# Attention outputs made as features: values, scores and transposes of three pairs in one stop of TensorE

## The chip, the cores and the metric

One NeuronCore of a Trainium2 chip runs the whole program in one launch. The metric is the device time in microseconds. The kernel before takes 2653.07 us (median of 3 runs, 2652.22 to 2653.91). TensorE is called PE here, VectorE DVE, ScalarE ACT, GpSimd POOL and the engine that issues the DMAs SP.

## The reference

Two transformer blocks run one after the other on 256 tokens with 2048 features. The first is a gated recurrence with convolutions and an MLP; the second, which most of the change touches, is

```
h = rms_norm(x, norm1_g)
aq, ak, av, bu, bg, cq, ck, cv = split(h @ w_in)            # 512 x5, 1024, 128, 128 columns
out_a = dilated_mixture(rms(aq), rms(ak), av)               # 8 heads of 64, each with its own keys and values
out_b = silu(layer_norm(causal_conv31(bu * sigmoid(bg))))   # 512 channels, 31 taps
out_c = band_attention(rms(cq), rms(ck), cv, sinks)         # 16 query heads, 2 key/value heads of 64
x = x + concat(out_a, out_b, out_c) @ w_out
x = x + (silu(rms_norm(x) @ w_gate) * (rms_norm(x) @ w_up)) @ w_down
```

An attention output is softmax(q k^T + mask) v for each head: o = P v / rowsum(P), where P is the exponential of the scores less their row maximum. The two LayerNorms of the first block are x -> (x - mean) * rstd * g + b over the 2048 features.

## The kernel before

Weights stream from HBM in pieces of 128 x 1024 numbers through a ring of four slots. Each float32 weight piece is split in two parts for the fast matmul: ACT writes the rounded upper part w_hi (L894, `split`), DVE the rest w_lo (L1365, `lo`), and PE multiplies both. A piece frees its slot when PE is done with it, and PE, ACT and DVE each have their order written out by hand, with semaphores between them.

The second block's attention runs beside the projections of `w_in` and `w_out`. Pieces of this part are numbered m = 0 to 59. For m = 0 to 43 a piece is 12 matmuls of 512 columns (L498 to L500); for m = 44 to 59 it is a `narrow_piece` of `w_out` (L831, L835), which reads the attention outputs. Before piece m each engine calls its own `beside(m)`, which holds the small work that has come due. The names to know are:

- `PAIRS`: 12 pairs of heads, eight of kind C (with sinks) and then four of kind A. Pair n is started at piece 16 + 3n (`PAIRS_AT`, `EVERY`), and `pair_at(m, late)` says which pair is due `late` pieces after its start.
- For a pair: `scores` on PE (late 0), `prepare` on DVE (late 0; adds the mask, takes the row maximum), `exps` on ACT (late 1), `transposes` on PE (late 3) and `turned_probs` on ACT (late 3), `values` on PE and `scale_out` on DVE (late 5), `turn_out` on PE and its split in mix_hi and mix_lo by ACT and DVE (late 7).
- `taps` on DVE: the 124 steps of the 31-tap convolution (31 for each of four tiles), spread over pieces 3 to 43 by `taps_by(m)`. At m = 44 DVE adds up the result (`part_of`, L1934, L1936), and PE sums it over the channels at m = 45 (`column_sum`, L618).
- `head_variance` and `norm_heads` on DVE at m and m + 1 for m in `HEADS_END` = 4, 12, 20, 28, 36; PE turns the normalised heads at m + 3 (L709) and has to wait for `norm_heads`.
- In the loop over m DVE does `scale_out`, then `lo` of piece m + 3, then `beside(m)`: first mix_lo, then `prepare`, the heads and the taps. Its queue is in order, so each of these stands behind the others.

The LayerNorms of the first block end on a chain PE (turns the normalised tiles, L600), DVE and ACT (gain and shift, `features` and `scaled`), ACT (`high`), DVE (`low`), PE (next matmul). While the chain runs PE does matmuls with zeros (`keep_busy`, L529).

## Time and profile before

| | |
|---|---|
| runs, median | 2653.07 us (2652.22 to 2653.91) |
| the profiled execution's own time | 2652.17 us |
| its span | 2650.4 us |
| granted TensorE clock | 0.999 |
| PE busy | 2640.4 us, 100% of the span |
| DVE busy | 1750.5 us, 66% |
| ACT busy | 1347.2 us, 51% |
| DMA | 494 MB, mean 186 GB/s |

The time of the profiled execution is 1.8 us above its span: what lies around it. Busy times are over the whole span; the stretches matter here, since the change touches some 200 us. In rows of a timeline the first number is a start in us from the span's beginning, the second how long the merged instructions took; a float32 matmul leaves two records, so six matmuls stand as x12 or as several rows of x2. Matmuls overlap, so the distance between two starts tells what one costs.

### The profile page before, as it was taken

What the parts mean: (1) busy time and instruction counts of PE and PEld (TensorE: products, weight loads), DVE (VectorE), ACT (ScalarE), POOL (GpSimd) and SP (SyncE); (2) the same over time, 40 slices, a digit from 0 to 9 for tenths busy, and PEclk for the clock granted to TensorE, in tenths of its full rate; (3) what the DMA queues carried; (4) which work ended last, traced back from release to release, by engine and by line L of the source; (5) the groups of instructions that cost most, each with busy time, mean ns of one, the idle gap of its engine ahead of it and who ended that gap; (6) DMA issues with size and microseconds to landing.
All of it is one profiled execution on the core that took longest, in us unless ns stands there. A gap on an engine that the chain in (4) does not pass through costs nothing.

```text
span 2650.4 us, 40578 instructions
## 1 busy us (share of the span) xinstructions
PE 2640.4 (100%) x14407; PEld 2291.4 (86%) x14407; DVE 1750.5 (66%) x1875; ACT 1347.2 (51%) x1540; POOL 36.6 (1%) x30
## 2 busy tenths in 40 slices
PE   9999999999999999999999999999999999999999
PEld 8888888888888888888888888889888888888888
DVE  7788877544454655555555568997666666666667
ACT  5767765444444544444444445566554444444444
POOL 0000000000000100000000001000100000000000
PEclk9999999999999999999999999999999999999999
DMA  7555555555555455555555554433555555555554
GB/s 266 182 186 188 187 189 192 200 181 190 202 195 199 165 183 195 178 191 200 194 178 193 199 191 157 168 136 136 175 191 187 188 189 189 190 190 190 190 190 167
DMA packets 133881, 494.01 MB, mean 186 GB/s; under 512 B 14864, under 2 KB 15376, under 8 KB 133776
## 3 DMA queue, kind: packets, MB, share of 16 engines
q1 hardware_dynamic: 133776, 492.62, 54.5%
q8 instruction: 65, 1.06, 0.2%
q14 instruction: 40, 0.33, 0.0%
HBM read 490.46 MB, written 2.10 MB: 186 GB/s over the span
## 4 chain that ended last, share of the span: by engine, by line
PE 95%; DVE 3%; issue 1%; ACT 1%; DMA 0%; DVEq 0%; SPq 0%; ACTq 0%
PE ps_b L389 18%; PE ps_a L389 18%; PE ps_b L400 10%; PE ps_a L400 10%; PE ps_b L498 6%; PE ps_b L500 6%; PE ps_b L499 6%; PE ps_a L498 5%; PE ps_a L499 5%; PE ps_a L500 5%; PE ps_b L831 1%; DVE w_lo L1365 1%; PE ps_b L835 1%; DVE bconv L1866 1%; DVE gates L1511 1%
## 5 line engine op out<-in xcount | busy, mean ns | idle before, releaser
L1365 DVE TENSOR_TENSOR w_lo<-w_raw,w_hi 128x1024 fp32r<-128x1024 f32 (+1 forms) x908 | 1120.6, 1251 | 731.7 <-ACT w_hi L894 722.1
L894 ACT ACTIVATE w_hi<-w_raw 128x1024 fp32r<-128x1024 f32 (+1 forms) x908 | 967.7, 1076 | 1130.1 <-PE ps_b L500 242.4
L389 PE MATMUL ps_b<-xx,w_hi 128*128 128x512 f32 x1184 | 288.6, 393 | 3.4 <-DVE xx L1682 1.8
L389 PE MATMUL ps_a<-xx,w_hi 128*128 128x512 f32 x1120 | 269.1, 391 | 0.0
L389 PEld LDWEIGHTS ps_b<-xx,w_hi 128*128 128x128 f32 x1184 | 217.6, 189 | 46.9 <-ACT w_hi L894 3.4
L389 PEld LDWEIGHTS ps_a<-xx,w_hi 128*128 128x128 f32 x1120 | 205.8, 188 | 39.9
L389 PE MATMUL ps_a<-x,w_hi 128*128 128x512 f32 x704 | 165.9, 390 | 0.0
L389 PE MATMUL ps_b<-x,w_hi 128*128 128x512 f32 x704 | 165.5, 390 | 0.0
L400 PEld LDWEIGHTS ps_b<-xx,w_lo 128*128 128x128 f32 x1184 | 152.8, 192 | 5.8
L400 PE MATMUL ps_b<-xx,w_lo 128*128 128x256 f32 x1184 | 155.5, 283 | 0.0
L389 PEld LDWEIGHTS ps_b<-x,w_hi 128*128 128x128 f32 x704 | 130.8, 188 | 26.2
L389 PEld LDWEIGHTS ps_a<-x,w_hi 128*128 128x128 f32 x704 | 130.6, 188 | 26.1
L400 PEld LDWEIGHTS ps_a<-xx,w_lo 128*128 128x128 f32 x1120 | 142.3, 191 | 4.8 <-DVE w_lo L1365 0.4
L400 PE MATMUL ps_a<-xx,w_lo 128*128 128x256 f32 x1120 | 144.7, 283 | 0.0
L498 PE MATMUL ps_b<-w_hi,xx 128*128 128x512 f32 (+1 forms) x320 | 124.0, 388 | 0.0
L500 PE MATMUL ps_b<-w_hi,xx 128*128 128x512 f32 (+1 forms) x320 | 121.5, 380 | 0.0
L499 PE MATMUL ps_b<-w_lo,xx 128*128 128x512 f32 (+1 forms) x320 | 121.4, 379 | 0.0
L498 PE MATMUL ps_b<-w_hi,ff 128*128 128x512 f32 x256 | 99.9, 390 | 0.0
L500 PE MATMUL ps_b<-w_hi,ff 128*128 128x512 f32 x256 | 99.6, 389 | 0.0
L499 PE MATMUL ps_b<-w_lo,ff 128*128 128x512 f32 x256 | 99.6, 389 | 0.0
L498 PE MATMUL ps_a<-w_hi,ff 128*128 128x512 f32 x256 | 99.6, 389 | 0.0
L499 PE MATMUL ps_a<-w_lo,ff 128*128 128x512 f32 x256 | 99.6, 389 | 0.0
(311 smaller groups left out, 3960.7 us busy)
## 6 DMA issues: line engine op xcount, KB each, us to landing
w_raw<-w_dram SPq DMA_DIRECT2D x836, 512.0 KB, 3.3
w_raw<-w_dram SPq DMA_DIRECT2D x72, 640.0 KB, 4.0
zz<-x_dram SPq DMA_DIRECT2D x8, 256.0 KB, 4.7
x_res<-x_dram SPq DMA_DIRECT2D x4, 512.0 KB, 4.6
out_dram<-res SPq DMA_DIRECT2D x3, 512.0 KB, 2.8
out_dram<-res SPq DMA_DIRECT2D x4, 128.0 KB, 2.1
const<-const_dram SPq DMA_DIRECT2D x1, 449.0 KB, 5.8
prm<-prm_dram SPq DMA_DIRECT2D x1, 308.0 KB, 5.4
```

What stands on the lines that cost most here:

```text
L389: last = nc.tensor.matmul(group[:, j, :], w_hi[:, r, o * P:o * P + P], moving(src, at + k), start=begins and k == 0, stop=not begins and k ...
L400: last = nc.tensor.matmul(group[:, j, 0:S], w_lo[:, r, o * P:o * P + P], moving(src, at + k)[:, 0:S], start=begins and k == 0, stop=not be ...
L498: nc.tensor.matmul(dst, x_hi, hi, start=k == 0 and not begun, stop=False)
L499: nc.tensor.matmul(dst, x_hi, lo, start=False, stop=False)
L500: last = nc.tensor.matmul(dst, x_lo, hi, start=False, stop=k == kt - 1)
L831: nc.tensor.matmul(banks[:, j // 2, (j % 2) * S:(j % 2) * S + S], w_hi[:, r, cols], mix_tile(k)[:, half_at:half_at + S], start=False, stop ...
L835: last = nc.tensor.matmul(banks[:, j // 2, (j % 2) * S:(j % 2) * S + S], w_lo[:, r, cols], mix_tile(k)[:, 0:S], start=False, stop=k == 3 a ...
L894: act.activation(w_hi[:, r, 0:width], w_raw[:, r, 0:width], ACT.Copy).then_inc(hi_done, 1)
L1365: dve.tensor_tensor(w_lo[:, r, 0:width], w_raw[:, r, 0:width], w_hi[:, r, 0:width].bitcast(F32), ALU.subtract).then_inc(lo_even if r % 2 = ...
L1511: own.done(dve.tensor_tensor_scan(gates[:, hd, way, 0, order], aa[:, way, hd, order], tt[:, way, hd, order], 0.0, ALU.mult, ALU.add))
L1866: ins = dve.scalar_tensor_tensor(y, x, column("cv_w", n), y, ALU.mult, ALU.add)
```

## The change

The attention outputs are made with features in the partitions, so they need no transpose after them. For that the probabilities are divided by their sum before they are turned (`scale_probs` on DVE replaces `scale_out`), and `values` takes the values as the stationary operand (128 keys x 64 features) and the turned probabilities as the moving one (128 columns). The two heads of a pair write partitions 0 to 63 and 64 to 127 of the last quarters of the banks GA 2 and GA 3; `turn_out`, the tile `on` and two semaphores go. On PE the values of pair n - 3, the scores of pair n and the transposes of pair n - 2 stand together, in one stop in three pieces (two later at the end: `values_at`). DVE does `scale_probs` and `prepare` before its `lo`. The taps are spread anew: none at pieces 12 to 14, 88 from piece 15 on, where there were 72 from piece 16 on. In the LayerNorms the transposes go in the order 0, 2, 1, 3 with a semaphore after tile 2 of the first block, ACT does its first `high` before its first `scaled`, and 4 of the 26 `keep_busy` matmuls that ran there go.

```diff
             turn_normed(0, 1)
-            keep_busy(4, GB[:, 0, :])
+            keep_busy(2, GB[:, 0, :])
...
-                    for j in range(SN):
+                    for j in (0, 2, 1, 3):
                         last = nc.tensor.transpose(normed_tile(b, j)[:, t * P:t * P + P], zt[:, t, b, j * P:j * P + P], ident)
+                        if (b, t, j) == (0, 1, 2):
+                            last.then_inc(first_turned, 1)
...
             turn_normed(1, 1)
-            keep_busy(5, GB[:, 0, :])
+            keep_busy(3, GB[:, 0, :])
...
+        def values_at(m):
+
+            n, last = pair_at(m, 9), pair_at(m, 8)
+            return last if last is not None and last >= 9 else n if n is not None and n < 9 else None
...
             def transposes(n):
-                pe.wait_ge(exp_done, n + 1)
+                pe.wait_ge(p_scaled, n + 1)
...
             def values(n):
-                for hd in range(2):
-                    part = slice(64 * hd, 64 * hd + 64)
-                    p_t = probs_t[:, n % 2, hd, :]
-                    nc.tensor.matmul(GA[:, 0, 64 * hd:64 * hd + 64], p_t[:, 0:P], vt[:, 0, v, part], start=True, stop=True)
...
+                for keys, block in ((0, 0), (0, 1), (1, 1)):
+                    at = (keys + block) * P
+                    for hd in range(2):
+                        part = slice(64 * hd, 64 * hd + 64)
+                        last = nc.tensor.matmul(GA[part, 2 + block, 3 * P:4 * P], vt[:, keys, v, part],
+                                                probs_t[:, n % 2, hd, at:at + P], start=keys == 0, stop=keys == block)
                 last.then_inc(o_psum, 1)
...
-                n = pair_at(m, 3)
-                if n is not None:
-                    transposes(n)
-                n = pair_at(m, 5)
+                n = values_at(m)
                 if n is not None:
                     values(n)
-                n = pair_at(m, 7)
-                if n is not None:
-                    turn_out(n)
                 n = pair_at(m, 0)
                 if n is not None:
                     scores(n)
+                n = pair_at(m, 6)
+                if n is not None:
+                    transposes(n)
...
             def first_blocks(n, q):
+                act.wait_ge(first_kept, n + 1)
+                high(n, 0, 1).then_inc(first_hi, 1)
                 act.wait_ge(norm_turned[n], 1)
                 scaled(n, 0, 1).then_inc(first_kept1, 1)
-                act.wait_ge(first_kept, n + 1)
                 act.wait_ge(first_kept1, n + 1)
-                high(n, 0, 1).then_inc(first_hi, 1)
...
-                return max(0, min(4 * TAPS2, 4 * (m - 2) if m < 16 else 52 + (72 * (m - 15) + 27) // 28))
+                return max(0, min(4 * TAPS2, 4 * (m - 2) if m < 12 else 36 if m < 15 else 36 + (88 * (m - 14) + 28) // 29))
...
-            def scale_out(n):
+            def scale_probs(n):
...
+                for blk, cols in ((0, slice(0, P)), (1, slice(P, 3 * P))):
+                    part = probs[:, b, :, cols]
+                    last = dve.tensor_tensor(part, part, rsum[:, b, blk, :].unsqueeze(2).to_broadcast(
+                        [P, 2, cols.stop - cols.start]), ALU.mult)
+                last.then_inc(p_scaled, 1)
...
             for m in range(MIX_END):
-                n = pair_at(m, 5)
+                n = pair_at(m, 2)
                 if n is not None:
-                    scale_out(n)
+                    scale_probs(n)
+                n = pair_at(m, 0)
+                if n is not None:
+                    prepare(n)
```

On PE, before, the work of pairs 2, 3 and 4 stands at three pieces in turn (values of 2 at piece 27, transposes of 3 and scores of 4 at 28, the turn of output 2 at 29), each between ordinary matmuls:

```order
L759 MATMUL ps_a<-vt,probs_t 128x64
L498 MATMUL ps_b<-w_hi,xx 128x512
...
L742 MATMUL ps_a<-const,probs 128x128 x6
L729 MATMUL ps_a<-ckt,cqt 128x128
L730 MATMUL ps_a<-ckt,cqt 128x256
L729 MATMUL ps_a<-ckt,cqt 128x128
L730 MATMUL ps_a<-ckt,cqt 128x256
L498 MATMUL ps_b<-w_hi,xx 128x512
...
L766 MATMUL ps_a<-const,on 128x128 x2
```

Of the change, the stop of PE at piece 28 (values of pair 1, scores of 4, transposes of 2) is

```order
L504 MATMUL ps_b<-w_hi,xx 128x512
L761 MATMUL ps_a<-probs_t,vt 64x128 x6
L733 MATMUL ps_a<-ckt,cqt 128x128
L734 MATMUL ps_a<-ckt,cqt 128x256
L733 MATMUL ps_a<-ckt,cqt 128x128
L734 MATMUL ps_a<-ckt,cqt 128x256
L746 MATMUL ps_a<-const,probs 128x128 x6
L502 MATMUL ps_b<-w_hi,xx 128x512
```

The three visits became one; the six value matmuls write 64 partitions and 128 columns where they wrote 128 and 64, and the two output transposes are gone.

DVE before, pieces 22 to 24 (w_lo is `lo`, probs<-ps_a and peak are `prepare`, bconv the taps, mixc the lower part of an output, rsum and on are `scale_out`):

```order
L1882 TENSOR_TENSOR probs<-ps_a,const 128x768
L1885 TENSOR_REDUCE peak<-probs 128x2
L1886 TENSOR_REDUCE peak<-probs 128x2
L1892 TENSOR_SCALAR negm<-peak,prm 128x2 x2
L1866 SCALAR_TENSOR_TENSOR bconv<-bpad,prm,bconv 128x256 x2
L1365 TENSOR_TENSOR w_lo<-w_raw,w_hi 128x1024
L1389 TENSOR_TENSOR mixc<-ps_a,mixc 128x256
L1866 SCALAR_TENSOR_TENSOR bconv<-bpad,prm,bconv 128x256 x3
L1900 TENSOR_TENSOR rsum<-rsum,sink 128x4
L1902 RECIPROCAL rsum<-rsum 128x4
L1907 TENSOR_TENSOR on<-ps_a,rsum 128x256
L1365 TENSOR_TENSOR w_lo<-w_raw,w_hi 128x1024
```

DVE of the change, from the end of piece 23 into piece 25:

```order
L1859 SCALAR_TENSOR_TENSOR bconv<-bpad,prm,bconv 128x256 x3
L1894 TENSOR_TENSOR rsum<-rsum,sink 128x4
L1896 RECIPROCAL rsum<-rsum 128x4
L1900 TENSOR_TENSOR probs<-probs,rsum 128x2x128
L1900 TENSOR_TENSOR probs<-probs,rsum 128x2x256
L1358 TENSOR_TENSOR w_lo<-w_raw,w_hi 128x1024
L1859 SCALAR_TENSOR_TENSOR bconv<-bpad,prm,bconv 128x256 x3
L1875 TENSOR_TENSOR probs<-ps_a,const 128x768
L1878 TENSOR_REDUCE peak<-probs 128x2
L1879 TENSOR_REDUCE peak<-probs 128x2
L1885 TENSOR_SCALAR negm<-peak,prm 128x2 x2
L1358 TENSOR_TENSOR w_lo<-w_raw,w_hi 128x1024
```

The division of 256 numbers in each partition became one of 768 in two instructions, `prepare` stands ahead of `lo`, and three taps stand in each piece where there were two or three.

## Rows read from the trace of the kernel before

**Rows 1.** The page: busy us (share of the span) and instructions
```profile
PE 2640.4 (100%) x14407; PEld 2291.4 (86%) x14407; DVE 1750.5 (66%) x1875; ACT 1347.2 (51%) x1540; POOL 36.6 (1%) x30
```
**Rows 2.** Windows, pieces 16 to 43 and 44 to 59: stretch, length, busy by engine, clock, DMA
```profile
1700.27:1808.90 108.63, 108.63 (x606) 88.65 (x605) 101.09 (x195) 71.40 (x148) 0.00 (x0) 1.00 0.41 144
1808.90:1867.33 58.43, 58.43 (x486) 57.05 (x485) 36.88 (x53) 34.27 (x58) 0.00 (x0) 1.00 0.40 139
```
**Rows 3.** Timeline of PE: the values of one pair (piece 21)
```profile
1716.40 0.39 PE L500 MATMUL ps_b<-w_hi,xx 128*128 128x512 f32 x1
1716.63 0.33 PE L756 MATMUL ps_a<-vt,probs_t 128*128 128x64 f32 x2
...
1718.20 0.39 PE L499 MATMUL ps_b<-w_lo,xx 128*128 128x512 f32 x1
```
**Rows 4.** Timeline of PE: transposes and scores (piece 22)
```profile
1720.74 0.82 PE L742 MATMUL ps_a<-const,probs 128*128 128x128 f32 x6
1721.48 0.50 PE L729 MATMUL ps_a<-ckt,cqt 64*128 64x128 f32 x4
1721.81 0.61 PE L730 MATMUL ps_a<-ckt,cqt 64*128 64x256 f32 x4
...
1722.69 0.40 PE L499 MATMUL ps_b<-w_lo,xx 128*128 128x512 f32 x1
```
**Rows 5.** Timeline of PE: the turn of an output (piece 26)
```profile
1737.69 0.38 PE L766 MATMUL ps_a<-const,on 128*128 128x128 f32 x2
...
1738.14 0.40 PE L499 MATMUL ps_b<-w_lo,xx 128*128 128x512 f32 x1
```
**Rows 6.** Timeline of DVE, pieces 22 to 24
```profile
1725.75 0.95 DVE L1882 TENSOR_TENSOR probs<-ps_a,const 128x768 f32<-128x768 f32 x1
...
1728.05 0.87 DVE L1866 SCALAR_TENSOR_TENSOR bconv<-bpad,prm,bconv 128x256 f32<-128x256 f32 x2
1728.84 1.22 DVE L1365 TENSOR_TENSOR w_lo<-w_raw,w_hi 128x1024 fp32r<-128x1024 f32 x1
...
1730.31 1.27 DVE L1866 SCALAR_TENSOR_TENSOR bconv<-bpad,prm,bconv 128x256 f32<-128x256 f32 x3
1731.50 0.15 DVE L1900 TENSOR_TENSOR rsum<-rsum,sink 128x4 f32<-128x4 f32 x1
...
1732.37 1.23 DVE L1365 TENSOR_TENSOR w_lo<-w_raw,w_hi 128x1024 fp32r<-128x1024 f32 x1
```
**Rows 7.** Timeline of DVE at pieces 12 and 13
```profile
1689.72 1.23 DVE L1365 TENSOR_TENSOR w_lo<-w_raw,w_hi 128x1024 fp32r<-128x1024 f32 x1
1690.85 1.22 DVE L1915 TENSOR_REDUCE hsum<-hsq 128x16 f32<-128x1024 f32 x1
...
1692.20 1.67 DVE L1866 SCALAR_TENSOR_TENSOR bconv<-bpad,prm,bconv 128x256 f32<-128x256 f32 x4
...
1694.92 0.25 DVE L1924 RECIPROCAL hrn<-hsd 128x16 f32<-128x16 f32 x1
...
1696.34 1.66 DVE L1866 SCALAR_TENSOR_TENSOR bconv<-bpad,prm,bconv 128x256 f32<-128x256 f32 x4
```
**Rows 8.** Timeline of PE: turn of the heads at piece 15, with its idle time
```profile
1696.48 1.09 PE L709 MATMUL ps_b<-const,hnb 128*128 128x128 f32 x8 [0.88 <-DVE hnb L1928]
```
**Rows 9.** Timeline of DVE at piece 44
```profile
1810.25 1.23 DVE L1365 TENSOR_TENSOR w_lo<-w_raw,w_hi 128x1024 fp32r<-128x1024 f32 x1 [0.38 <-ACT w_hi L894]
```
**Rows 10.** Timeline of PE: the column sum at piece 45
```profile
1813.71 0.65 PE L618 MATMUL ps_a<-bpart,ones 128*128 128x256 f32 x2
```
**Rows 11.** Timeline of ACT: its first gain and shift in the second LayerNorm
```profile
1600.88 0.56 ACT L1071 ACTIVATE res<-ps_a,prm 128x256 f32<-128x256 f32 x1 [0.58 <-PE ps_a L600]
```
**Rows 12.** Timeline of PE in the second LayerNorm: zero matmuls, and a wait behind them
```profile
1601.47 1.34 PE L529 MATMUL ps_b<-zero 128*128 128x512 f32 x5
1602.71 0.70 PE L389 MATMUL ps_b<-xx,w_hi 128*128 128x512 f32 x2
...
1611.23 0.47 PE L389 MATMUL ps_b<-xx,w_hi 128*128 128x512 f32 x1 [1.81 <-DVE xx L1682]
```

More of the change, by code:

```diff
@@ L225, in build @@
             sem(n) for n in ("score_psum", "score_out", "peak_ready", "exp_done"))
-        pt_psum, pt_out, o_psum, o_scaled, o_turned = (
-            sem(n) for n in ("pt_psum", "pt_out", "o_psum", "o_scaled", "o_turned"))
+        p_scaled, pt_psum, pt_out, o_psum = (sem(n) for n in ("p_scaled", "pt_psum", "pt_out", "o_psum"))
         mix_hi, mix_lo = sem("mix_hi"), sem("mix_lo")
@@ L737, in transposes @@
                 if n >= 2:
-                    pe.wait_ge(mix_lo, n - 1)
+                    pe.wait_ge(mix_lo, n - 1 if n < 10 else n)
                 for hd in range(2):
@@ L747, in values @@
                 pe.wait_ge(pt_out, n + 1)
-                pe.wait_ge(score_out, min(n + 2, 12))
                 if n >= 1:
-                    pe.wait_ge(o_scaled, n)
+                    pe.wait_ge(mix_lo, n)
                 if n in (0, 8):
                     pe.wait_ge(v_kept, 1 + (n == 8))
-                for hd in range(2):
-                    part = slice(64 * hd, 64 * hd + 64)
-                    p_t = probs_t[:, n % 2, hd, :]
-                    nc.tensor.matmul(GA[:, 0, 64 * hd:64 * hd + 64], p_t[:, 0:P], vt[:, 0, v, part], start=True, stop=True)
-                    dst = GA[:, 0, P + 64 * hd:P + 64 * hd + 64]
-                    nc.tensor.matmul(dst, p_t[:, P:2 * P], vt[:, 0, v, part], start=True, stop=False)
-                    last = nc.tensor.matmul(dst, p_t[:, 2 * P:3 * P], vt[:, 1, v, part], start=False, stop=True)
-                last.then_inc(o_psum, 1)
-            def turn_out(n):
-                pe.wait_ge(o_scaled, n + 1)
-                pe.wait_ge(pt_out, min(n + 2, 12))
-                for blk in range(2):
-                    last = nc.tensor.transpose(GA[:, 2, blk * P:blk * P + P], on[:, blk, :], ident)
-                last.then_inc(o_turned, 1)
+                for keys, block in ((0, 0), (0, 1), (1, 1)):
[4 more added lines that the diff above has]
+                                                probs_t[:, n % 2, hd, at:at + P], start=keys == 0, stop=keys == block)
+                last.then_inc(o_psum, 1)
             def beside(m):
@@ L1250, in beside @@
                     keep_values(V_END, slice(0, 4), GB[:, 0:2, :])
-                n = pair_at(m, 7)
-                if n is not None:
-                    hi_of(mixed(n)[:, 0:S], GA[:, 2, 0:S], o_turned, n + 1, mix_hi)
-                n = pair_at(m, 3)
+                n = pair_at(m, 6)
                 if n is not None:
                     turned_probs(n)
+                n = values_at(m)
+                if n is not None:
+                    hi_of(mixed(n)[:, 0:S].rearrange("p (b t) -> p b t", b=2), GA[:, 2:4, 3 * P:4 * P], o_psum, n + 1, mix_hi)
                 if m in HEADS_END:
@@ L1666, in features @@
             def features(n, b, tiles):
-                dve.wait_ge(norm_turned[n], b + 1)
+                dve.wait_ge(*((first_turned, n + 1) if b == 0 else (norm_turned[n], b + 1)))
                 for j in tiles:
@@ L1938, in beside @@
             def beside(m):
-                n = pair_at(m, 7)
+                n = values_at(m)
                 if n is not None:
-                    lo_of(mixed(n)[:, S:2 * S], GA[:, 2, 0:S], mixed(n)[:, 0:S], n + 1, mix_hi, mix_lo)
-                n = pair_at(m, 0)
-                if n is not None:
-                    prepare(n)
+                    parts = mixed(n).rearrange("p (h b t) -> p h b t", h=2, b=2)
+                    lo_of(parts[:, 1, :, :], GA[:, 2:4, 3 * P:4 * P], parts[:, 0, :, :], n + 1, mix_hi, mix_lo)
                 if m in HEADS_END:
@@ L1985, in _ @@
             for m in range(MIX_END):
-                n = pair_at(m, 5)
+                n = pair_at(m, 2)
                 if n is not None:
-                    scale_out(n)
+                    scale_probs(n)
+                n = pair_at(m, 0)
+                if n is not None:
+                    prepare(n)
                 if m == B_VAR_AT - 1:
```

15 lines of the change are left out of this document (3 added, 12 removed).

## The prediction

> **What bounds the kernel now.** I read the page's busy times first, then windows over the stretch that the change touches, then the timelines of PE and DVE in it. PE is busy for the whole span [rows 1], so outside the attention a change pays only if it takes time from PE. In pieces 16 to 43 PE is busy for all of 108.63 us, but DVE for 101.09 of them [rows 2]: two engines are near their limit there, and one must not be read without the other. In pieces 44 to 59 DVE has 36.88 of 58.43 us [rows 2] and is no limit. That DVE already ends a wait shows at piece 15: PE stands 0.88 us until DVE has normalised the heads [rows 8].
>
> **PE, stop by stop.** An ordinary matmul costs 0.23 (1716.40 to 1716.63) [rows 3]. The values of a pair cost 1718.20 - 1716.63 - 0.23 = 1.34 us, 0.112 for each of 12 records. Transposes and scores together cost 1722.69 - 1720.74 - 0.23 = 1.72, of which the scores 1722.69 - 1721.48 - 0.23 = 0.98 [rows 4]. The turn of an output costs 1738.14 - 1737.69 - 0.23 = 0.22 [rows 5]. A pair has 3.28.
>
> After the change transposes and scores stay 1.72 (the same two changes of array shape, in another order), and the turn goes. New is the price of the values with two column halves, which no row shows. The nearest rows are the scores: two heads in two halves of the rows. In the program their matmuls alternate, in the timeline the four short records start together at 1721.48 and the four long ones at 1721.81 [rows 4], so the heads run beside each other. Their records hold 1536 columns; the transposes pay 0.108 to 0.12 for 128, so one after the other they would need 1.3 us, and they take 0.98 with both changes of shape. Two at a time is 0.65, and 0.33 is left for going in and out. So values, two at a time: 6 x 0.112 + half of 0.33 = 0.83. Lower bound 0.65 (no change of shape); upper bound, one after another with each load of 64 columns (half of 0.112) in the open: 12 x (0.108 + 0.056) + 0.16 = 2.1. I take 0.83, by its nearest row. PE then gains 1.34 + 0.22 - 0.83 = 0.73 a pair, 8.8 for twelve, and 0.9 if the wait at piece 15 goes.
>
> The Trainium skill ("TensorEngine Tiling (Array Packing)", Key Properties) says that tiles load and multiply independently and that changing the mode drains the array; the trace agrees with both in the scores (0.33 for two changes). Its page "TensorE: Matmul & The Clock Gate" (Part 3, The mechanism) speaks against this change: a weight load overlaps running matmuls only where the row group differs, and matmuls start strictly in program order. Column halves share their rows; by that rule the loads would stand in the open, and the price would be near my upper bound. The row of the scores already contradicts the order half of it.
>
> **DVE, the same stretch.** Prices [rows 6, 7]: `lo` 1.13 (1689.72 to 1690.85); a tap 0.396 (three from 1730.31 to 1731.50); `prepare` 2.30 (1725.75 to 1728.05); mix_lo 0.34 (1728.84 to 1730.31 less `lo`); `scale_out` 0.87 (1731.50 to 1732.37); head variance 1.35 (1690.85 to 1692.20); head norm 1.42 (1694.92 to 1696.34). `scale_probs` isn't in the trace. It keeps the sum and reciprocal (0.40) and has two products in SBUF of 256 and 512 numbers: a tile of 256 costs 0.34 as mix_lo, and `lo` with 1024 costs 1.13, so (1.13 - 0.34) / 768 = 1.03 ns a number and 0.34 + 0.60. Together 1.34; bounds 1.2 (no fixed part in the second) and 1.6 (twice 0.4 more of waiting between dependent steps).
>
> DVE's queue from `lo` at piece 12 (1689.72) to the end of the channel sum at piece 44, after the change: 33 `lo` 37.3; 124 - 36 = 88 taps 34.8; 10 `prepare` 23.0; 9 `scale_probs` 12.1; 7 mix_lo 2.4; 4 variances 5.4; 4 norms 5.7; channel sum 1.1. That is 121.8, and 1.3 of waiting (0.9 at piece 15, where it would overtake ACT's w_hi, and 0.3 for the first scores): it ends at 1812.8. PE's column sum of piece 45 needs it. It ran at 1813.71 [rows 10]. PE alone would be there about 9.6 earlier, at 1804 (0.9 of idle time, eight turns 1.8, nine values at 1.34 against seven at 0.83, one set of transposes 0.65 later). So nearly all that PE saves is waited away again, first where PE turns the heads: piece 23 about 1, piece 31 about 3.5, piece 39 about 2.5 and the column sum about 2, 9 in all. What grows on DVE are 12 taps more from piece 16 on (4.8), 0.47 a pair for the scaling, and one pair scaled earlier. Behind a late DVE on PE stand all later pieces. First stretch: -0.9.
>
> The same list with the durations of before ends 1.7 us too early at piece 44 (1808.6 by the list, 1810.25 in the row [rows 9]), since DVE also waits for ACT, 0.38 there. With more in its queue it waits less; I take half, +0.8.
>
> **From the column sum to the end of piece 59.** PE is the limit. Five values fall here (pairs 7 to 11) where three did: 5 x 0.83 - 3 x 1.34 = +0.1. One set of transposes more, +0.65, four turns less, -0.9. The second column sum (piece 48) needs the squares of the centred convolution. `values` no longer stands before it, and `prepare` of piece 46 now follows values and scores on PE before DVE reaches the subtraction, about 1.1 later: I estimate a wait of 0.8. Sum +0.7. The output of pair 7 is made at piece 46 and multiplied at 47; DVE needs prepare, lo and mix_lo for it, about as long as PE has: nothing, but up to 2 us if DVE is behind.
>
> **The LayerNorms.** ACT's first step waited for PE's last transpose (1600.88 [rows 11]). Now DVE starts two transposes earlier (0.22) and ACT waits for its first tile, 0.22 less but 0.54 and 0.07 more, so ACT's row begins at 1601.27, 0.39 later, with all of its work behind. The first matmul (1602.71) comes about 0.3 earlier, and two of the five zero matmuls (0.22 each) [rows 12] make room for that. In the second LayerNorm PE stands at 1611.23 after 1.81 of idle time, behind DVE and ACT [rows 12]: the 0.39 arrives there in full, and the 0.3 is only a longer wait. In the first one PE has no such wait within reach and keeps 0.3. Sum +0.1.
>
> **Sum.** -0.9 + 0.8 + 0.7 + 0.1 = +0.7 on the profiled execution's 2652.17: 2652.9. The median of the runs lies 0.9 above that execution, so 2653.8. Changes below 0.2% (5.3 us) can't be told from none here.
>
> **Rivals.**
> - DVE keeps up. Then PE keeps 8.8 + 0.9, less a few tenths: about 2644. For it: in pieces 16 to 43 DVE had 7.5 us to spare, and it begins piece 16 some 4 us earlier since four rounds of taps have moved. Against it: the list above is 1 to 2 us too short when tried on the kernel before. 15%.
> - The column halves don't run beside each other, loads in the open: a values stop at 2.1. Until piece 44 this is mostly hidden in waits for DVE (7 x 1.27 = 8.9 against 9 of waits); from the column sum on it decides, 5 x 1.27 = 6.4, about 2660. 12%. One after the other with hidden loads (1.50 a stop) is 2657 and counts with my forecast's case.
> - The stop is too late for its consumers: DVE arrives at pieces 46 to 48 still behind, so the output of pair 7 and the squares come late and PE stands 3 us more before pieces 47 and 48, and the heads' turn at 31 and 39 pays each microsecond of DVE's excess (scaling at 1.6 instead of 1.34 gives 3 more). Point of decision: a DVE queue that ends past 1816. 2660 to 2662. 8%.
> - The forecast, DVE takes what PE gives: 65%, own range 2650 to 2658.
>
> Range: 2646 to 2661, which takes in both bounds for the values' price and for the scaling. Faster by over 0.2%: the first rival and a little of the forecast's case, 0.17. Slower: 0.16. Within: 0.67.
>
> **What the changed profile would show.** Right: values stops of about 0.8 us with the two heads' records starting together; DVE busy near 100% in pieces 20 to 43; idle time of PE before L715 (the turn of the heads) released by DVE, some 2 to 4 us at pieces 31 and 39, and before the column sum; PE's busy time down by about 9 us with the span unchanged. In the second LayerNorm the wait of 1.81 grows to about 2.5. Wrong: no idle time of PE at the heads (then the first rival), values records one after another, 1.3 us or more a stop (the second), or ACT instead of DVE as the releaser, which no term of mine holds.

## The result: 0.16% slower, inside the 0.2% that the forecast called no change

The changed kernel takes 2656.66 us (median of 21 runs, 2654.15 to 2658.15), the kernel before 2652.22 on the same chip (21 runs, 2650.88 to 2654.37). The ratio is 1.0016, with an interval of 1.0010 to 1.0022, which in time is 2.7 to 5.8 us. The forecast was 2653.8 with a range of 2646 to 2661, and "within 0.2%" at 0.67. The interval leaves out zero: the change is slower, by little. In the difference to the kernel before, the forecast was +0.7 us and the result is +4.4. PE's busy time fell, by 6.3 us where about 9 was forecast, and the time did not.

The page of the changed kernel, busy us, share of the span and instructions (the same line of before is [rows 1]; the span is 2654.5, before 2650.4):

```profile
PE 2634.1 (99%) x14379; PEld 2280.8 (86%) x14379; DVE 1757.2 (66%) x1887; ACT 1347.0 (51%) x1540; POOL 36.1 (1%) x30
```

PE has 6.3 us less to do, DVE 6.7 more. The windows of pieces 16 to 43 and 44 to 59, with the columns of [rows 2] (the third number from the end is the granted clock):

```profile
1700.05:1811.26 111.21, 103.98 (x574) 82.08 (x573) 108.06 (x213) 71.42 (x147) 0.00 (x0) 0.97 0.38 133
1811.26:1871.45 60.19, 57.66 (x493) 54.73 (x492) 38.76 (x55) 35.04 (x59) 0.00 (x0) 1.00 0.41 141
```

In the first, PE was busy for all of 108.63 us before and is now idle for 7.2 of 111.21; DVE is busy for 108.06. The list of PE's waits from 1700 to 1871 us (who waits, for whom; us in total, times, longest) names the places:

```profile
PE ps_b L715 <- DVE hnb L1920: 7.2, 3, 3.7
PE ps_a L746 <- DVE xx L1382: 1.4, 1, 1.4
PE ps_a L624 <- DVE bpart L1928: 1.1, 2, 0.7
```

L715 is the turn of the heads, L746 the transposes, L624 the column sum. Before, the only wait of PE in the attention was the one of [rows 8].

A stop with all three parts in PE's timeline of the changed kernel, at piece 25, and the first column sum, at piece 45 (the first column is the start, the second the length of the merged records):

```profile
1731.18 0.88 PE L761 MATMUL ps_a<-probs_t,vt 128*64 128x128 f32 x12
1731.98 0.50 PE L733 MATMUL ps_a<-ckt,cqt 64*128 64x128 f32 x4
1732.31 0.61 PE L734 MATMUL ps_a<-ckt,cqt 64*128 64x256 f32 x4
1732.85 0.87 PE L746 MATMUL ps_a<-const,probs 128*128 128x128 f32 x6
...
1815.11 0.67 PE L624 MATMUL ps_a<-bpart,ones 128*128 128x256 f32 x2 [0.39 <-DVE bpart L1928]
```

The twelve records of the values take 1731.98 - 1731.18 = 0.80 us, against 1.34 in [rows 3]. The whole stop, from the ordinary matmul before it to the second one behind it less two ordinary ones, is 2.48 us. The column sum starts 1.40 later than in [rows 10]; the changed profile was already 0.87 behind when the attention began, so the attention itself has cost 0.53 by then.

**Where the 4.1 us between the two spans lie.** Starts of the same pieces in both traces, subtracted:

| stretch | after - before, us |
|---|---|
| start to the first LayerNorm, unchanged code | +2.38 |
| first LayerNorm | -0.23 |
| second LayerNorm, its waits | +0.28 |
| second LayerNorm, a clock drop that only the profile of before has | -1.56 |
| attention, piece 0 to the column sum of piece 45 | +0.53 |
| from the column sum to piece 60 | +2.73 |
| piece 60 to the end | 0.0 |

The first row is chance: in the eleven kernels below the same code lies between -0.2 and +2.6 us from before's. What belongs to the change is the attention's 3.26 and 0.05 for the LayerNorms. That lies inside the interval of the timed difference. By a clock drop I mean a stretch at a granted clock of 0.50, 1.2 of 2.4 GHz; the changed profile has two of them in the attention, at pieces 31 and 39.

### The profile page after: what moved, and what is told of

It is laid out like the page before. It is cut to its first block, busy times and chain, and to the rows that moved or that the text cites. A ratio compares the mean times of both kernels' runs of the same rounds, so it can differ in the third digit from the quotient of the medians.

```text
span 2654.5 us, 40498 instructions
## 1 busy us (share of the span) xinstructions
PE 2634.1 (99%) x14379; PEld 2280.8 (86%) x14379; DVE 1757.2 (66%) x1887; ACT 1347.0 (51%) x1540; POOL 36.1 (1%) x30
## 4 chain that ended last, share of the span: by engine, by line
PE 91%; DVE 6%; issue 1%; ACT 1%; DMA 1%; SPq 0%; DVEq 0%; ACTq 0%
PE ps_a L393 18%; PE ps_b L393 18%; PE ps_a L404 10%; PE ps_b L404 9%; PE ps_b L502 6%; PE ps_b L503 6%; PE ps_b L504 6%; PE ps_a L503 5%; PE ps_a L502 5%; PE ps_a L504 5%; DVE w_lo L1358 2%; PE ps_b L824 1%; DVE bconv L1859 1%; DMA w_raw<-w_dram 1%; DVE gates L1504 1%
```

## The experiments

All were compared with the kernel before on the same chip; the median of before was 2652.07 in the first four, 2652.39 in the next, 2652.37 in the last three. "Attention" is the time from piece 0 to piece 60 in the profile, less the 213.60 of before; the changed kernel has +3.26.

### The two parts alone

`ln_only` is the kernel before with the LayerNorm edits, `attn_only` the changed kernel without them:

```
-                    for j in (0, 2, 1, 3):          # attn_only: back to range(SN),
+                    for j in range(SN):             # no first_turned, keep_busy(4) and (5)
```

> The kernel before with only the LayerNorm part of the change (two zero matmuls fewer in each, the transposes of the first tile group in the order 0, 2, 1, 3, DVE released two transposes earlier, ACT's high part ahead of its scaling). Theory: worth +0.1 us, 0.3 gained in the first LayerNorm and 0.39 lost in the second, where the wait of 1.81 at L393 grows to about 2.3; against the kernel before 0.0 to +0.5. The 2.3 us that the profiled execution of the changed kernel lies behind by 255 us from its start, where the two programs are alike, is then chance and need not show here. Rival: the LayerNorm edits carry a large part of the 4 us of the changed kernel: +1.5 or more. Second rival: since the profile of before shows a granted clock of 0.50 for 3.4 us behind the 1.81 wait and the changed one does not, the edits avoid it and gain 1.6: about -1.4.

> The changed kernel with the LayerNorm part taken back: only the attention part of the change. Theory: the attention carries all of it: pieces 0 to 60 take 3.3 us more than before (0.5 up to the column sum of piece 45, 2.7 behind it), PE stands about 1.6, 3.7 and 2.0 us before the turn of the heads at pieces 23, 31 and 39; the time is that of the changed kernel within 0.5 us, 3 to 4 above the kernel before. Rival: the attention edits alone are neutral and the LayerNorms carry the loss: within 1 us of the kernel before.

Measured: `ln_only` 2652.55 us, ratio 1.0002 (0.9993 to 1.0011); `attn_only` 2655.97, ratio 1.0015 (1.0006 to 1.0025), attention +3.42. The LayerNorms are worth nothing, the attention carries all. In `ln_only` the first LayerNorm gains 0.27 and the second loses 0.28, the signs that were forecast and nearly the sizes (0.3 and 0.39). The second rival fell: its profile has the clock drop behind the wait, although the LayerNorms are those of the changed kernel; `attn_only`, with the LayerNorms of before, has none. So the drop doesn't belong to the edits.

### Is DVE the bound, and what is it worth

`act_scale` moves the two products of `scale_probs` to ACT, `fewer_taps` leaves out 48 taps of the convolution:

```
 DVE, scale_probs(n):
-                own.done(dve.reciprocal(rsum[:, b, :, :], rsum[:, b, :, :]))
-                ... two tensor_tensor products, then_inc(p_scaled, 1)
+                dve.reciprocal(rsum[:, b, :, :], rsum[:, b, :, :]).then_inc(r_ready, 1)
 ACT, three pieces after the scores:
+                for hd in range(2):
+                    for blk, cols in ((0, slice(0, P)), (1, slice(P, 3 * P))):
+                        last = act.activation(probs[:, b, hd, cols], probs[:, b, hd, cols], ACT.Copy,
+                                              scale=rsum[:, b, blk, hd:hd + 1])
```

> The changed kernel, but the two products of scale_probs (0.34 and 0.60 expected, about 1.0 measured together) are done by ACT, as four activations with the reciprocal as their scale (about 1.8 us of ACT a pair, which has 40 us to spare in pieces 16 to 43); DVE keeps the sum and the reciprocal. Theory (DVE's queue sets the pace up to the column sum): DVE is relieved of 9 x 1.0 us there, the waits of PE before the turn of the heads (7.2 in all) and before the column sums fall to under 2 together, PE's saving of 7 to 9 us comes through: 5 to 8 us less than the changed kernel, about 2649 to 2651. Rival 1 (DVE is only late by where its steps stand, not by their sum): the waits stay within 2 us of 7.2 and the time is unchanged. Rival 2: ACT becomes late with w_hi or the turned scores: new waits of PE or DVE for ACT, 2656 or more.

```
 taps():
+                    if 10 <= k < 22:
+                        continue
```

> The changed kernel, with the taps 10 to 21 of the convolution's 31 left out on all four tiles (48 of 124 taps of 0.396 us, 19 us of DVE; the convolution's result is another one). Nothing else is touched, PE and ACT have the same work. Theory (DVE is the bound up to the column sum): all waits of PE before the turn of the heads go (7.2) and most of the 1.1 before the column sums and the 1.4 at piece 52; PE's own saving shows undiminished: about 9 us less than the changed kernel, 2647 to 2649, and 5 less than the kernel before. Rival (PE's stops cost more than reckoned, DVE is not the bound): less than 3 us under the changed kernel.

Measured: `act_scale` 2648.00 us, ratio 0.9981 (0.9972 to 0.9990), attention -5.56, which is 8.8 less than the changed kernel. `fewer_taps` 2650.37, ratio 0.9994 (0.9985 to 1.0003), attention -2.98. PE's waits in `act_scale`, in the stretch from 1695 to 1875 us:

```profile
PE ps_b L716 <- DVE hnb L1928: 2.6, 3, 1.5
PE ps_a L625 <- DVE bpart L1936: 1.1, 2, 0.7
PE ps_a L747 <- DVE xx L1396: 0.3, 1, 0.3
```

1.0 us a pair taken from DVE takes 4.6 from the heads' waits and 1.1 from the one at piece 52. The other 3.1 of the 8.8 are no wait: PE ran through two clock drops in the changed kernel's attention and through none here. That does not make them a gift of the clock. Counted on DVE, from `lo` at piece 12 to the channel sum, the queue fell from 124.4 to 116.7 us, by 9.2 of work less 1.5 of more idle time, and 7.7 of the 8.8 are that. The gain is above the 5 to 8 us expected, while the waits stayed at 3.7 together where under 2 was expected. ACT pays 1.49 us for four activations. PE never waits for it; DVE does twice, 0.57 us each, for w_hi:

```profile
1733.78 0.38 ACT L903 ACTIVATE mixc<-ps_a 128x256 fp32r<-128x256 f32 x1
1734.04 1.49 ACT L1215 ACTIVATE probs<-probs,rsum 128x128 f32<-128x128 f32 x4
1735.90 1.06 ACT L888 ACTIVATE w_hi<-w_raw 128x1024 fp32r<-128x1024 f32 x1 [0.37 <-PE ps_b L505]
```

`fewer_taps` missed its 9 us: it gained 6. Its waits:

```profile
PE ps_b L715 <- DVE hnb L1922: 2.9, 2, 2.0
PE ps_a L624 <- DVE bpart L1930: 2.5, 2, 1.7
PE ps_a L746 <- DVE xx L1382: 1.4, 1, 1.4
```

DVE has 19 us less to do, but the taps left out are the middle ones in the order of time, so DVE has 16.2 us of idle time in pieces 12 to 44 and is still late for the last heads and the column sum, behind the full rounds of taps at the end. The wait at piece 52 does not move at all. Two things follow: DVE's queue is the bound, and the sum over the stretch is not enough; where in the stretch the work stands counts as well. The next two test that.

### Where DVE's steps stand

`old_taps` puts the convolution's taps where they were before the change; `mix_first` moves one step:

```
 taps_by(m), old_taps:
-    4 * (m - 2) if m < 12 else 36 if m < 15 else 36 + (88 * (m - 14) + 28) // 29
+    4 * (m - 2) if m < 16 else 52 + (72 * (m - 15) + 27) // 28
 DVE's loop over the pieces, mix_first:
+                if values_at(m) == 9:
+                    keep_output(m)            # the low part of pair 9's output, no longer behind lo()
                 n = pair_at(m, 2)
                 if n is not None:
                     scale_probs(n)
```

> The changed kernel with the convolution's taps on the pieces as before: 16 more by piece 15 (4 a piece up to there) and 16 fewer from piece 15 to 43. Theory (DVE's whole queue from piece 12 on sets the column sum; the schedule only shifts where it is late): the wait at piece 15 of PE for the heads' norm comes back (0.9), the waits at pieces 23 and 31 shrink by about 1.5 and 2, all together the same queue, so the column sum comes at the same time within 0.7 us and so does the end. Rival (taps cost only where they stand in the heads' way): the waits at 23, 31 and 39 fall from 7.2 to under 3 and the kernel is 3 us faster than the changed one.

> The changed kernel, with one step moved on DVE: at piece 51 it makes the low part of pair 9's output before it scales pair 11 and before the weights' low part, not behind both. Theory: the 1.41 us that PE stands at piece 52 before the transposes are the price of that order; the step then ends near the high part that ACT ends at 1842.5, PE's wait falls to 0.3 or less, and as DVE has 1 to 3 us to spare in each piece there nothing else grows: 1.2 to 1.5 us less than the changed kernel, about 2655. Rival: the time comes back before piece 60, for instance as a wait for pair 11's transposes or for a later low part; within 0.5 us of the changed kernel.

Measured: `old_taps` 2652.97 us, ratio 1.0002 (0.9993 to 1.0012), attention +0.21: the time is the rival's, 3.05 less than the changed kernel; the sum of the waits, 6.8, is nearly unchanged as the theory had it, but the one at piece 23 grew from 1.62 to 2.23 where it should have shrunk. PE stands at four turns of the heads instead of three, the longest 2.46 instead of 3.66; here pieces 15 and 31:

```profile
1698.27 1.09 PE L715 MATMUL ps_b<-const,hnb 128*128 128x128 f32 x8 [0.88 <-DVE hnb L1920]
...
1757.70 1.09 PE L715 MATMUL ps_b<-const,hnb 128*128 128x128 f32 x8 [2.46 <-DVE hnb L1920]
```

The explanation is in DVE's idle time over pieces 12 to 44 (all gaps, summed): 8.2 us before, 4.1 in the changed kernel, 1.6 in `old_taps`. The changed table leaves pieces 12 to 14 without taps, so DVE then waits for ACT and for the first scores at pieces 15, 16 and 18. With 16 taps there it doesn't, and its queue is 3.0 us shorter, 2.5 of it idle time. Of these 2.5 the three waits of pieces 15, 16 and 18 are 2.0 (0.83, 0.56 and 0.60). The fourth, of 0.43, stands behind the first clock drop and belongs to it rather than to the taps: see below. My expectation reckoned the queue's work and forgot that the schedule decides how much of the idle time is filled.

`mix_first` took 2654.34 us, ratio 1.0008 (0.9999 to 1.0017), attention +1.76, 1.5 less than the changed kernel, all of it between pieces 45 and 60 (54.73 against 56.34). DVE and PE at pieces 51 and 52 of `mix_first`:

```profile
1841.49 0.42 DVE L1382 TENSOR_TENSOR xx<-ps_a,xx 128x256 fp32r<-128x256 f32 x1 [0.19 <-ACT xx L902]
1841.83 0.17 DVE L1896 RECIPROCAL rsum<-rsum 128x4 f32<-128x4 f32 x1
1842.03 1.03 DVE L1900 TENSOR_TENSOR probs<-probs,rsum 128x256 f32<-128x256 f32 x2
1842.98 1.22 DVE L1358 TENSOR_TENSOR w_lo<-w_raw,w_hi 128x1024 fp32r<-128x1024 f32 x1
```

```profile
1842.48 0.82 PE L746 MATMUL ps_a<-const,probs 128*128 128x128 f32 x6
```

The same place in the changed kernel:

```profile
1845.09 0.84 PE L746 MATMUL ps_a<-const,probs 128*128 128x128 f32 x6 [1.41 <-DVE xx L1382]
```

The transposes of pair 10 wait for the semaphore of pair 9's low part (`mix_lo`, which `transposes` wants at n - 1 for the earlier pairs and at n from pair 10 on); in the changed kernel the scaling of pair 11 and the weights' low part stood ahead of it. The transposes write the first three quarters of the two banks, and the outputs stand in the last. For the earlier pairs the transposes run before the output made in the same stop has been read (at piece 25 they start at 1732.85, and ACT reads it at 1734.47). So the data in the quarters don't explain why the count is one higher from pair 10 on. Whether the wait can simply be left out was not tried. The low part moved by one place gives 1.5 us in the profile and 2.5 in the medians, whose intervals overlap.

### The price of two column halves

`one_half` writes both heads to partitions 0 to 63, head after head, so the second head overwrites the first:

```
-                for keys, block in ((0, 0), (0, 1), (1, 1)):
-                    for hd in range(2):
-                        last = nc.tensor.matmul(GA[part, 2 + block, 3 * P:4 * P], ...
+                for hd in range(2):
+                    for keys, block in ((0, 0), (0, 1), (1, 1)):
+                        last = nc.tensor.matmul(GA[0:64, 2 + block, 3 * P:4 * P], ...
```

> The changed kernel, but both heads' value matmuls write partitions 0 to 63, head after head (three records of one, then three of the other), so that no two records lie in different column halves; the second head overwrites the first, so the outputs of the heads are other ones. Number and shape of the records are the same. Theory (the 0.80 us of a values stop come from two column halves at a time): a values stop takes 12 x 0.112 + 0.16 = 1.5 us, the pitch of the records is near 0.11 each with no pairs 6 ns apart. Up to piece 44 the 7 x 0.7 us are hidden in PE's waits for DVE, from the column sum on 5 x 0.7 = 3.5 are not: about 3.5 us over the changed kernel, 2659 to 2661. Rival 1 (records of 64 columns are cheap by themselves, half of the columns to load and no overlap of halves): a stop stays at 0.8 and the time is unchanged. Rival 2 (weight loads stand in the open when both use the same rows and columns): 2.1 a stop, 6 us or more over the changed kernel.

```profile
1732.90 1.52 PE L761 MATMUL ps_a<-probs_t,vt 128*64 128x128 f32 x12
1734.36 0.50 PE L733 MATMUL ps_a<-ckt,cqt 64*128 64x128 f32 x4
```

The stop takes 1734.36 - 1732.90 = 1.46 us, against 0.80 with both halves: the same twelve records, of the same shape. The halves do run beside each other, and the loads are hidden in both cases (rival 2 would need 2.1). The edit changes the order too, head after head, so that the order alone could undo the overlap is not excluded; the price of going one at a time is shown either way. The kernel took 2657.89 us, ratio 1.0021 (1.0012 to 1.0030), attention +5.06. That is 1.8 over the changed kernel in the profile, not 3.5: 2.6 more after the column sum (58.92 against 56.34), since the wait at piece 52 gave 0.6 back, and 0.8 less before it, where PE's waits took in the seven longer stops (4.9 at the heads instead of 7.2) and no clock drop fell in the attention. DVE's program is the same there, so this pair of profiles prices the drops as well (below).

### The scaling on GpSimd

`pool_scale` is `act_scale` with the two products as tensor_tensor on GpSimd.

> The changed kernel, with the two products of scale_probs on GpSimd, which has nothing to do in the attention; DVE keeps the sum and the reciprocal. Its own rows cost 1.6 us for 256 numbers and 2.8 for 1024, so about 1.6 + 1.9 = 3.5 us a pair, of the 8.2 that lie between a pair's scaling and its transposes. Theory: DVE is relieved of 1.0 us a pair as with ACT, the waits at the heads fall from 7.2 to about 2.6, and the time is within 1 us of the 2648 that ACT gave. Rival 1: GpSimd takes DVE's access to memory while it works, DVE's rows beside it grow (the low part over 1.13, a tap over 0.40) and eat the relief: 2654 or more. Rival 2: the transposes come before GpSimd is done, PE stands for POOL at L746.

Measured: 2654.36 us, ratio 1.0009 (1.0000 to 1.0019), attention +2.61. Rival 1. GpSimd and DVE in its trace:

```profile
1730.13 2.70 POOL L2086 TENSOR_TENSOR probs<-probs,rsum 128x256 f32<-128x256 f32 x2 [8.45 <-DVE rsum L1897]
```

```profile
1729.97 1.21 DVE L1359 TENSOR_TENSOR w_lo<-w_raw,w_hi 128x1024 fp32r<-128x1024 f32 x1
1731.10 2.41 DVE L1860 SCALAR_TENSOR_TENSOR bconv<-bpad,prm,bconv 128x256 f32<-128x256 f32 x3
...
1737.19 1.27 DVE L1860 SCALAR_TENSOR_TENSOR bconv<-bpad,prm,bconv 128x256 f32<-128x256 f32 x3
```

Three taps take 2.41 us beside GpSimd's products and 1.27 without them: DVE gets 1.0 us of relief a pair and loses up to 1.1. In the profile 0.65 us is left of the gain: the column sum comes 1.1 earlier, the wait at piece 52 fell from 1.41 to 0.33 as in `act_scale`, and a clock drop at piece 45 takes about 1.5 back. The `lo` that was already running when GpSimd began was not slowed. Once, at piece 48, GpSimd began while DVE stood idle; then its two products took 1.61 instead of 2.70, and the `lo` that came behind them 2.00 instead of 1.21:

```profile
1827.46 1.61 POOL L2086 TENSOR_TENSOR probs<-probs,rsum 128x256 f32<-128x256 f32 x2 [13.13 <-DVE rsum L1897]
```

```profile
1828.15 2.00 DVE L1359 TENSOR_TENSOR w_lo<-w_raw,w_hi 128x1024 fp32r<-128x1024 f32 x1 [0.77 <-ACT w_hi L888]
```

The Trainium skill ("SBUF — State Buffer", SBUF: two separate sides) says that a GpSimd instruction that reads SBUF and a DVE instruction with two SBUF inputs exclude each other, and that whoever starts first holds the shared ports for the whole instruction. The rows agree in both halves.

### Together, and the clock

`tuned` is the changed kernel with the LayerNorms of before, `old_taps` and `mix_first`; `tuned_act` has ACT's scaling too; `tuned_act_awake` also fills one wait of PE:

```
 need_normed(n), before the wait at the second quarter:
+                    if n == 1 and k == 4:
+                        for _ in range(8):
+                            nc.tensor.matmul(GB[:, 0, :], zero ... , start=False, stop=False)
```

> The changed kernel with the LayerNorm part taken back, the taps on the pieces as before, and pair 9's low part ahead of pair 11's scaling; DVE still does all of the scaling. Theory (the losses are separate and each of the size that its own run showed): the taps' table 3.0, the order at piece 51 1.6, the LayerNorms 0.3, together 4.9 less than the changed kernel's 2656.7, so 2651 to 2652.5, about 0.5 under the kernel before. Rival (the early taps and the moved low part take from the same slack of DVE): one of the two is lost, 2653 or more.

> The same, with the two products of the scaling on ACT as in the run before that did so. Theory: ACT's 8.8 for pieces 0 to 60, less 0.3 for the LayerNorms and 0.3 at piece 52, which had 0.3 of wait left; PE's wait at the heads was 2.6 there and falls by about 1.5 with the early taps: 2645.5 to 2646.5, 6 under the kernel before. Rival: with ACT's relief DVE is no limit any more and the early taps give nothing but the wait at piece 15 (0.9): 2648 or more.

> The same again, and in the second LayerNorm eight matmuls by zero (8 x 0.22 us, added to a bank that is being summed, so nothing changes in it) fill the 1.8 us that PE stands before L393. Theory: the halved granted clock that 6 of 10 profiles show for 3.4 us right behind that wait, 1.56 us each time, is answered by PE's idleness; with the wait filled the clock stays at full speed there in the profile, and the mean time falls by about 6/10 x 1.6 = 0.9 against the kernel without the filling. Rival: the clock falls there all the same, or the matmuls delay the ones behind them: same time or up to 0.5 more.

| kernel | us | ratio to before | attention |
|---|---|---|---|
| `tuned` | 2651.23 | 0.9994 (0.9985 to 1.0003) | -0.09 |
| `tuned_act` | 2646.82 | 0.9977 (0.9968 to 0.9986) | -5.70 |
| `tuned_act_awake` | 2645.64 | 0.9973 (0.9963 to 0.9984) | -5.64 |

`tuned` is 5.4 under the changed kernel where the parts sum to 4.9, so the losses are separate. Its profile shows only 3.35 of it; 1.3 of the rest is a clock drop, priced below. `tuned_act` is 0.1 under `act_scale` in the profile and 1.2 in the median. The moved low part gives 0.5 there (54.73 against 55.23 from the column sum on), so the early taps cost 0.4 (153.18 against 152.81 up to it): with the scaling on ACT the wait of 0.88 at piece 15 comes back, and the heads' waits hardly fall, 2.6 to 2.4, where 1.5 less was expected. On that point the rival was right. What the old taps would do without the moved part was not run. `tuned_act_awake` is the best kernel of this study, 6.7 us under the one before. Its second LayerNorm, in PE's timeline:

```profile
1609.04 1.91 PE L619 MATMUL ps_b<-zero 128*128 128x512 f32 x8
1611.01 2.08 PE L394 MATMUL ps_b<-xx,w_hi 128*128 128x512 f32 x8
```

The kernel before, same place:

```profile
1611.23 3.40 PE L389 MATMUL ps_b<-xx,w_hi 128*128 128x512 f32 x8 [1.81 <-DVE xx L1682]
1614.43 1.39 PE L400 MATMUL ps_b<-xx,w_lo 128*128 128x256 f32 x8
```

Eight matmuls take 2.08 us in the one and 3.40 in the other. The windows over those 3.4 us, with the granted clock as the third number from the end; before, then filled:

```profile
1611.23:1614.63 3.40, 3.40 (x9) 2.69 (x10) 3.40 (x6) 3.29 (x6) 0.00 (x0) 0.56 0.20 57
```

```profile
1611.00:1614.40 3.40, 3.39 (x21) 3.06 (x22) 3.40 (x6) 3.31 (x6) 0.00 (x0) 1.00 0.22 78
```

The difference in the medians, 1.2 us, is near the 0.9 expected, but the intervals of the two kernels overlap. The timed runs of the experiments and of the changed kernel come with a mean granted clock, to three decimals: a profile with a drop reads 0.999, the one without reads 1.000. All eight runs of `tuned_act_awake` read 1.000, and six of ten of `tuned_act`; of 89 runs of the kernel before, 55 read 1.000 and 34 read 0.999, and the 34 are 1.5 to 1.7 us slower in the mean of each group. Four of ten against none of eight makes it likely, not certain, that the filling keeps the drop away. The price of some 1.6 us shows in the times too. Of the 21 runs of the changed kernel none reads 1.000.

## Why the prediction was right, and where its parts were not

**DVE takes what PE gives: right.** DVE had no gap over 0.1 us in pieces 19 to 43 but one of 0.43; PE stood 1.62, 3.66 and 1.95 us at pieces 23, 31 and 39 where 1, 3.5 and 2.5 were forecast, released by DVE, and `act_scale` turned 1.0 us a pair off DVE into 8.8 us. The first rival ("DVE keeps up", about 2644) is the direction in which the kernel goes once DVE is relieved.

**The queue's length: right in size.** From `lo` at piece 12 to the column sum the changed trace has 124.5 us: 122.1 of work and small gaps (list: 121.8) and 2.4 of waits over 0.06 us (list: 1.3, and 0.8 added by the calibration). That the 0.8 came near is luck. By the prediction's own prices the list of before reaches `lo` of piece 44 at about 1804.2 (32 `lo` 36.2, 88 taps 34.8, 10 `prepare` 23.0, 8 `scale_out` 7.0, 7 mix_lo 2.4, variances and norms 11.1), not at 1808.6. That is 6.1 before the row, and the trace has 6.5 us of waits in between. The "1.7 us too early", of which the 0.8 is half, is not what the sum gives, and no row shows it. The scaling was 1.34 as forecast:

```profile
1732.67 0.15 DVE L1894 TENSOR_TENSOR rsum<-rsum,sink 128x4 f32<-128x4 f32 x1
1732.86 0.18 DVE L1896 RECIPROCAL rsum<-rsum 128x4 f32<-128x4 f32 x1
1733.07 1.02 DVE L1900 TENSOR_TENSOR probs<-probs,rsum 128x256 f32<-128x256 f32 x2
1734.01 1.22 DVE L1358 TENSOR_TENSOR w_lo<-w_raw,w_hi 128x1024 fp32r<-128x1024 f32 x1
```

What was forecast for the column sum was -0.9 + 0.8 = -0.1; it came at +0.53, 0.3 by work and 0.3 by waits. Two clock drops of 3.4 us lie in that stretch of the changed profile, at the waits of pieces 31 and 39, and no term of the prediction held them. What a drop costs depends on whether DVE feels it. `tuned` and `old_taps` have the same program up to piece 50 but for the LayerNorms; one has a drop at the wait of piece 31, the other none. From piece 16 to the column sum they take 112.26 and 110.94. The 1.3 reach DVE as a wait in front of its next scaling; the second row is the same place in the changed kernel:

```profile
1768.44 0.16 DVE L1892 TENSOR_TENSOR rsum<-rsum,sink 128x4 f32<-128x4 f32 x1 [1.23 <-ACT sink L1203]
```

```profile
1768.77 0.16 DVE L1894 TENSOR_TENSOR rsum<-rsum,sink 128x4 f32<-128x4 f32 x1 [0.43 <-ACT sink L1205]
```

There the two drops together cost less: `one_half`, with the same program on DVE and no drop in the attention, has no such wait, and its queue is 0.8 us shorter (PE's stops are longer in it, so this is an estimate). The rest of what PE loses in the drops it would have spent waiting for DVE.

**The values stop: right.** 0.80 against 0.83, with the two heads beside each other; `one_half` shows the alternative at 1.46. With all twelve records in the same rows and columns (`one_half`), they still start 0.11 us apart, so the loads are hidden there too. The Trainium skill ("TensorE: Matmul & The Clock Gate", Part 3, The mechanism) says that a load overlaps running matmuls only where the row group differs, and that matmuls start in program order. By the first the prediction reckoned with a price near its upper bound of 2.1, and no run shows one. The second does not hold in the scores: the program has short, long, short, long, and the four short records start before the four long ones.

**PE's saving a pair in the first stretch was near the forecast,** 0.81 instead of 0.73: the three parts took 1.34 + 1.72 + 0.23 = 3.29 before and 2.48 now. Scores followed by transposes, where they stand without values (piece 22), take 1.67, against the 1.72 of transposes followed by scores [rows 4], so the order hardly matters. As PE waits there anyway, it made no difference. That PE's busy time fell by 6.3 and not by 9 is in part the clock: the changed profile has two drops of 3.41 us and that of before one, so about 1.7 us more of PE's time is matmuls at half the clock (an estimate from these lengths).

**The second stretch failed: +2.73 against +0.7.** PE's stops behind the column sum came out at +0.5, where the terms said -0.15: 10.5 us in eight stops against 10.0 in ten, each taken less two of the neighbouring matmuls of 0.12. The values carry most of that. With scores and transposes behind them they add 0.80, but in the three stops where they stand alone they take 1.00, since the change of array shape is then paid for them alone, in and out; the five cost 4.6, not 5 x 0.83 = 4.15. The wait for the squares at piece 48 was 0.73 against 0.8. The larger part is the step on the outputs, which failed: "The output of pair 7 is made at piece 46 [...] nothing, but up to 2 us if DVE is behind". I followed pair 7's output into the product and none into the transposes, which wait for its low part by a semaphore. The one on the path was pair 9's, at piece 51, and not because DVE was behind (it is busy for 38.76 of the 60.19 us of these sixteen pieces): one step stood last in its order. It is 1.4 us, and `mix_first` gives it back. Waits and stops together make 2.66 of the 2.73.

**The LayerNorms: right.** The ACT row that starts the second one begins at 1603.39 - 2.15 (the offset there) = 1601.24, forecast 1601.27, and the wait of [rows 12] grew from 1.81 to 2.31, where about 2.5 was forecast:

```profile
1603.39 0.51 ACT L1071 ACTIVATE xx<-res,prm 128x256 fp32r<-128x256 f32 x1 [0.94 <-DVE res L1664]
```

```profile
1613.66 2.08 PE L393 MATMUL ps_b<-xx,w_hi 128*128 128x512 f32 x8 [2.31 <-DVE xx L1675]
```

The gain of 0.2 in the first and the loss of 0.28 in the second cancel, and `ln_only` shows nothing in 11 runs.

**What made it miss.** In the attention it is 2.7 us, 3.26 against +0.6: 1.4 for pair 9's low part, 0.7 for PE's stops in the second stretch, 0.6 for the first stretch, of which the two drops can hold all (0.8). The difference of the medians missed by 3.7, so 1.0 more lies outside what the two profiles of the attention show. The granted clock is a candidate and not shown to be all of it: the forecast started from a profile of before that holds one drop, while 55 of 89 timed runs of that kernel read 1.000 and none of the 21 of the changed kernel does. That the absolute time missed 2653.8 by only 2.9 is luck: the three runs from which the forecast took "0.9 above" have a median 0.85 over that of the 21.

## What to carry to other kernels

When PE and a second engine are both near their limit in a stretch, price an edit on both, and add up the second one's queue with its idle time: the schedule of work that could stand anywhere (here the taps) decides how much of the idle time is filled, and cost 3.0 us here. When an edit moves outputs, follow each of them to every semaphore that another step waits for, not only the first one into its product. Price a stop both in company and alone: the change of array shape is paid once for all that stands together. Then look for an engine with time to spare whose work does not slow the second one's: a tap kept its 0.48 us throughout `act_scale` and took up to 1.26 beside GpSimd, and moving the same two products gave 8.7 us on ACT and 2.3 on GpSimd (medians; 8.8 and 0.65 in the profiles of the attention).

## What the runs showed of the hardware

- **Behind a wait of 1.8 to 2.3 us on PE the granted clock was often halved, not always.** At the end of the wait in the second LayerNorm or just behind it, 7 of 12 profiles show a granted clock of 0.50 (1.2 of 2.4 GHz) for 3.41 us: before, `ln_only`, `act_scale`, `fewer_taps`, `one_half`, `old_taps`, `tuned_act`. The other five, with the same wait, have no drop there, and each of them has one or two at a later wait (pieces 31 to 45, of 1.86 to 3.80 us) instead; the seven have none there, with waits up to 2.46. `tuned_act_awake`, where the first wait is filled, has none until the last microseconds. A drop cost 1.56 us where PE was the limit (second LayerNorm) and 1.3 in `tuned`'s attention, and two in the changed kernel's about 0.8 together, where DVE was the limit; two profiles must be compared with that in mind.
- **The drops were as long where PE was busy again at once.** In the changed kernel, at the turns of the heads, PE has work for nearly all of the 3.41 us (the third number from the end is the granted clock):

```profile
1755.99:1759.40 3.41, 3.13 (x20) 2.71 (x20) 3.34 (x9) 0.00 (x0) 0.00 (x0) 0.50 0.35 131
1790.12:1793.53 3.41, 3.41 (x13) 3.02 (x14) 3.41 (x8) 2.04 (x2) 0.00 (x0) 0.50 0.31 99
```

- **DVE's taps and GpSimd exclude each other** (three taps 1.27 us alone, 2.41 beside GpSimd), and so do `lo` and GpSimd. GpSimd's two products took 2.70 behind a running `lo` and 1.61 with DVE idle, where DVE itself took 0.94.
- **Column halves run beside each other in float32, and the change of shape is paid once for a stop:** twelve records take 0.80 us in two halves and 1.46 in one; a stop of values alone costs 1.00, with scores and transposes behind them they add 0.80. Scores then transposes cost 1.67, transposes then scores 1.72.
